# A constant starting address for the second block's activations, with 260 columns in its mixing and gate/value products

## What is computed

```
# block one, 256 positions
h    = rms_norm(x, norm1_w)
proj = h @ w_in                        # "in1": q, k, v, z, xbc, dt
x   += concat(attention, ssm) @ w_out  # "out1"
x   += conv_ffn(rms_norm(x, norm2_w))  # "ffn1": w_up 2048 x 11264, w_down 5632 x 2048
# block two, 16 meta positions ahead of the 256: 272 positions
z    = rmsnorm(h, g_pre_mix) @ w_in_2  # "in2"
mix  = concat(short_conv(z), rwkv7_scan(z)) @ w_out_2     # "out2"
h    = h + rmsnorm(mix, g_post_mix)
gate, up = split(rmsnorm(h, g_pre_ffn) @ w_gate_up)       # "ffn2"
f    = (silu(conv3(gate)) * up) @ w_down
out  = (h + rmsnorm(f, g_post_ffn))[:, 16:]
```

## Time and profile before

| | |
|---|---|
| runs | 2490.72, 2490.09, 2489.69 us; median 2490.09 |
| profiled execution | 2490.57 us, of which the instructions span 2488.8 us |
| TensorE matmul / weight load busy | 2470.6 us (99%) / 2379.1 us (96%) |
| VectorE / ScalarE / GpSimd busy | 1662.9 us (67%) / 1205.5 us (48%) / 59.5 us (2%) |
| granted TensorE clock | 0.999 of full speed |

### The profile page before, as it was taken

The page is one execution under the profiler, slowest core; times in us unless marked ns, Lnnn a source line. Parts: engine busy times, 40 slices in busy tenths (PEclk is TensorE's granted clock), DMA queues, the critical chain, the costliest instruction groups (busy, mean ns, idle before and its releaser), DMA issues.

```text
span 2488.8 us, 61026 instructions
## 1 busy us (share of the span) xinstructions
PE 2470.6 (99%) x25716; PEld 2379.1 (96%) x25716; DVE 1662.9 (67%) x2174; ACT 1205.5 (48%) x1450; POOL 59.5 (2%) x69
## 2 busy tenths in 40 slices
PE   9999999999999999999999999999999999999999
PEld 9989999999999999999999999999999999999997
DVE  7776667677777777788856655667656666556666
ACT  6646545555555555455523333346444444444444
POOL 0000000000000000004100000001000000000000
PEclk9999999999999999999999999999999999999999
DMA  7545556666666665666533333354655555655553
GB/s 229 163 145 156 150 166 191 198 193 193 192 193 191 189 197 187 190 193 176 160 107 103 104 96 105 111 170 153 208 181 185 182 181 176 190 181 185 179 182 129
DMA packets 397851, 420.57 MB, mean 169 GB/s; under 512 B 15422, under 2 KB 372530, under 8 KB 397554
## 3 DMA queue, kind: packets, MB, share of 16 engines
q1 hardware_dynamic: 397170, 416.46, 54.3%
q10 hardware_dynamic: 528, 1.84, 0.2%
HBM read 416.15 MB, written 2.10 MB: 168 GB/s over the span
## 4 chain that ended last, share of the span: by engine, by line
PE 96%; DVE 2%; ACT 1%; issue 1%; POOL 0%; ACTq 0%; POOLq 0%
PE psum L2572 26%; PE psum L2573 26%; PE psum L2574 26%; PE psum L2588 3%; PE psum L2587 3%; PE psum L2586 3%; PE psum L3050 2%; PE psum L3156 1%; PE psum L3146 1%; PE psum L3275 0%; DVE w_lo L1378 0%; PE psum L3197 0%; PE psum L3281 0%; PE psum L2818 0%; PE psum L2997 0%
## 5 line engine op out<-in xcount | busy, mean ns | idle before, releaser
L2572 PE MATMUL psum<-act_hi,w_hi 128*128 128x256 f32 (+3 forms) x4736 | 1350.1, 285 | 3.7 <-DVE act_lo L1416 2.9
L2573 PE MATMUL psum<-act_lo,w_hi 128*128 128x256 f32 (+3 forms) x4736 | 1333.5, 282 | 0.0
L2574 PE MATMUL psum<-act_hi,w_lo 128*128 128x256 f32 (+3 forms) x4736 | 1332.5, 281 | 0.3 <-issue 0.3
L1378 DVE TENSOR_TENSOR w_lo<-raw,w_hi 128x1024 fp32r<-128x1024 f32 x788 | 961.2, 1230 | 475.6 <-ACT w_hi L750 474.5
L750 ACT ACTIVATE w_hi<-raw 128x1024 fp32r<-128x1024 f32 x788 | 829.2, 1057 | 908.5 <-PE psum L2574 764.0
L2572 PEld LDWEIGHTS psum<-act_hi,w_hi 128*128 128x128 f32 x4736 | 894.1, 189 | 12.0 <-issue 3.5
L2573 PEld LDWEIGHTS psum<-act_lo,w_hi 128*128 128x128 f32 x4736 | 895.9, 189 | 3.6 <-issue 2.2
L2574 PEld LDWEIGHTS psum<-act_hi,w_lo 128*128 128x128 f32 x4736 | 894.3, 189 | 0.0
L2573 PE MATMUL psum<-ff_lo_rows,w_hi 128*128 128x256 f32 x640 | 176.8, 276 | 0.0
L2574 PE MATMUL psum<-ff_hi_rows,w_lo 128*128 128x256 f32 x640 | 176.8, 276 | 0.0
L2572 PE MATMUL psum<-ff_hi_rows,w_hi 128*128 128x256 f32 x640 | 176.8, 276 | 0.0
(11 more groups left out here) (431 smaller groups left out, 1926.9 us busy)
## 6 DMA issues: line engine op xcount, KB each, us to landing
raw<-in_w_in SPq DMA_DIRECT2D x188, 512.0 KB, 3.8
raw<-in_w_up SPq DMA_DIRECT2D x176, 512.0 KB, 4.5
raw<-in_w_down SPq DMA_DIRECT2D x176, 512.0 KB, 3.6
raw<-in_w_gate_up SPq DMA_DIRECT2D x176, 512.0 KB, 3.5
raw<-in_w_out SPq DMA_DIRECT2D x64, 512.0 KB, 3.5
x_rows<-in_x SPq DMA_DIRECT2D x8, 256.0 KB, 6.9
out_x<-out_rows SPq DMA_DIRECT2D x8, 256.0 KB, 2.6
raw<-in_w_in SPq DMA_DIRECT2D x4, 384.0 KB, 3.4
```

The lines of the kernel that those rows point to most:

```text
L1378: dve.tensor_tensor(w_lo[:, slot], raw[:, slot], w_hi[:, slot].bitcast(F32), ALU.subtract).then_inc(S["lo_done"], 1)
L2572: pe.matmul(out_, wh, xh, start=first and r == 0, stop=False)
L2573: pe.matmul(out_, wh, xl, start=False, stop=False)
L2574: mm = pe.matmul(out_, wl, xh, start=False, stop=last and r == RK - 1)
```

## The change

The rows of the activations in block two are put 1280 bytes (320 columns, `ROW2`) apart in buffers of their own, `act2_hi` and `act2_lo`, which start at a multiple of 256. Columns 4 to 275 hold the 272 positions. `LEAD` goes from 2 to 4, so that out2 and ffn2 work on 260 columns, which start at the same byte as in2's 260. The value half of ffn2 reads and computes the same 260 columns; `leave` takes 256 of them out of PSUM at an offset of 4. in1 and ffn1 share buffers `act1_hi` and `act1_lo` with rows 1024 bytes apart, begun at 64. The activations of the feed-forward parts all start at the head of their buffers. To find the room, `p1` to `p4` become one tile that is updated in place, and eight small tiles of the scan (`l2`, `l2t`, `l4`, `l4t`, `l8`, `lp`, `pn`, `tt`) lie in the 48 unused columns behind each activation row, so that their four pieces of 32 columns are 1280 bytes apart and no longer joined. No wait is added or taken away, and no instruction either.

```diff
-    LEAD = 2
+    LEAD = 4
...
+    ROW2 = 320
...
-    act_hi = sb("act_hi", [P, KD * T2 + 64], F32R)
-    act_lo = sb("act_lo", [P, KD * T2 + 64], F32R)
...
-    IN1_HI, IN1_LO = act_rows(44, T1)
-    FFN1_HI, FFN1_LO = act_rows(48, T1)
-    IN2_HI, IN2_LO = act_rows(4, T2)
-    MIX_HI, MIX_LO = [t[:, :, 0:T3] for t in act_rows(0, T2)]
...
+    sb("act_pad", [P, 56])
+    block1 = ExitStack()
+    M.update(shared([("act1_hi", [KD * T1 + 64], F32R), ("act1_lo", [KD * T1 + 64], F32R)], block1))
...
-         ("ssm_pad", [40], F32), ("ssm_hi", [8, T1], F32R), ("ssm_lo", [8, T1], F32R)],
+         ("ssm_pad", [48], F32), ("ssm_hi", [8, T1], F32R), ("ssm_lo", [8, T1], F32R)],
...
+    block2 = ExitStack()
+    M.update(shared([("act2_hi", [KD, ROW2], F32R), ("act2_lo", [KD, ROW2], F32R)]))
+    M.update(shared([("gap_hi", [KD, ROW2], F32), ("gap_lo", [KD, ROW2], F32)], block2))
...
-    FF_AT = dict(ffn1=0, ffn2=32)
...
-    LAST_HI, LAST_LO = [M[t][:, 2:2 + 4 * T1].rearrange("p (k t) -> p k t", t=T1)
-                        for t in ("last_hi_rows", "last_lo_rows")]
+    def act_rows(name):
+
+        return M[name][:, 16:16 + KD * T1].rearrange("p (k t) -> p k t", t=T1)
+
+    IN1_HI, IN1_LO = act_rows("act1_hi"), act_rows("act1_lo")
+    FFN1_HI, FFN1_LO = IN1_HI, IN1_LO
+    IN2_HI, IN2_LO = M["act2_hi"][:, :, 4:4 + T2], M["act2_lo"][:, :, 4:4 + T2]
+    MIX_HI, MIX_LO = IN2_HI[:, :, TC3], IN2_LO[:, :, TC3]
...
+    for at, names in enumerate((("l2", "l2t", "l4", "l4t"), ("l8", "lp", "pn", "tt"))):
+        for g, n in enumerate(names):
+            M[n] = M[("gap_hi", "gap_lo")[at]][:, 4 * g:4 * g + 4, 4 + T2:4 + T2 + RC]
...
-            def bank_pair(pair, T, rows_=P):
-                return psum[0:rows_, 2 * pair:2 * pair + 2, 0:T]
+            def bank_pair(pair, T, rows_=P, at=0):
+                return psum[0:rows_, 2 * pair:2 * pair + 2, at:at + T]
...
-                vals = [t[:, :, T - T1:T] for t in xs]
...
-                        if by_rows and j >= 2:
-                            group(v + 4 * j, g + j, (pair0 + j) % 2, vals, T1)
-                        else:
-                            group(v + 4 * j, g + j, (pair0 + j) % 2, xs, T)
+                        group(v + 4 * j, g + j, (pair0 + j) % 2, xs, T)
...
-                        unit(u + 12 + k, k, 3, *vals, 4 * k, T1, k == 0, k == 3)
+                        unit(u + 12 + k, k, 3, *xs, 4 * k, T, k == 0, k == 3)
...
-                    dve.tensor_tensor(M["p2"][0:RB], four(4, 2 * P), M["p1"][0:RB], ALU.add) \
+                    dve.tensor_tensor(M["p"][0:RB], four(4, 2 * P), M["p"][0:RB], ALU.add) \
```

More of the change, by code:

```diff
@@ L275, in two_blocks @@
     first.close()
+    block1.close()
+    block2 = ExitStack()
+    M.update(shared([("act2_hi", [KD, ROW2], F32R), ("act2_lo", [KD, ROW2], F32R)]))
+    M.update(shared([("gap_hi", [KD, ROW2], F32), ("gap_lo", [KD, ROW2], F32)], block2))
+    for names in (
+        [("packs", [NPACK, P], F32), ("x_rows", [2, D], F32), ("meta_rows", [D], F32)],
+        [
+            ("up", [8, T3], F32), ("conv", [8, T1], F32), ("ff", [4, T1], F32),
+            ("squares2", [8, T2], F32), ("row_pad", [48], F32),
+            ("ff_hi_rows", [4 * T1 + 64], F32R), ("ff_lo_rows", [4 * T1 + 64], F32R),
+            ("last_hi_rows", [4 * T1 + 64], F32R), ("last_lo_rows", [4 * T1 + 64], F32R),
+            ("out_rows", [2, D], F32),
+            ("row_ss", [2, 8], F32),
+        ],
+    ):
+        M.update(shared(names))
     both = ExitStack()
@@ L284, in two_blocks @@
     M.update(shared([
-        *[(n, [4, RC], F32) for n in ("ldt", "lo", "rbt0", "rbt1", "akt", "rkt0", "rkt1", "ld", "l2", "l2t", "l4",
-                                      "l4t", "l8", "p1", "p2", "p3", "p4", "lp", "pn", "tt")],
+        *[(n, [4, RC], F32) for n in ("ldt", "lo", "rbt0", "rbt1", "akt", "rkt0", "rkt1", "ld", "p")],
         ("rhs", [4, P], F32), ("trb", [12 * RC], F32),
@@ L297, in two_blocks, with rows_of_four @@
     both.close()
-    FF_AT = dict(ffn1=0, ffn2=32)
[L301 to L305, removed]
-    LAST_HI, LAST_LO = [M[t][:, 2:2 + 4 * T1].rearrange("p (k t) -> p k t", t=T1)
-                        for t in ("last_hi_rows", "last_lo_rows")]
+    block2.close()
+    def act_rows(name):
[4 more added lines that the diff above has]
+    MIX_HI, MIX_LO = IN2_HI[:, :, TC3], IN2_LO[:, :, TC3]
+    NORM_HI = dict(n0=IN1_HI, n1=FFN1_HI, n2=IN2_HI, n4=MIX_HI)
+    NORM_LO = dict(n0=IN1_LO, n1=FFN1_LO, n2=IN2_LO, n4=MIX_LO)
+    for at, names in enumerate((("l2", "l2t", "l4", "l4t"), ("l8", "lp", "pn", "tt"))):
+        for g, n in enumerate(names):
+            M[n] = M[("gap_hi", "gap_lo")[at]][:, 4 * g:4 * g + 4, 4 + T2:4 + T2 + RC]
+    def rows_of_four(name):
+        return M[name][:, 0:4 * T1].rearrange("p (k t) -> p k t", t=T1)
+    FF_HI, FF_LO = rows_of_four("ff_hi_rows"), rows_of_four("ff_lo_rows")
+    LAST_HI, LAST_LO = rows_of_four("last_hi_rows"), rows_of_four("last_lo_rows")
     proj = M["proj"]
@@ L1020, in while_up @@
                     hi_group(v + 8)
-                    product_hi(i - 1, v, ff_rows(name)[0])
+                    product_hi(i - 1, v, FF_HI)
                     hi(v + 12, 0)
@@ L1383, in lo_group, with leave @@
                     lo(u + j, j)
-            def bank_pair(pair, T, rows_=P):
-                return psum[0:rows_, 2 * pair:2 * pair + 2, 0:T]
-            def leave(u_end, pair, dst, T, rows_=P, how="scaled", single=False, t0=0):
+            def bank_pair(pair, T, rows_=P, at=0):
+                return psum[0:rows_, 2 * pair:2 * pair + 2, at:at + T]
+            def leave(u_end, pair, dst, T, rows_=P, how="scaled", single=False, t0=0, at=0):
                 dve.wait_ge(S["unit_used"], u_end)
-                src = bank_pair(pair, T, rows_)
+                src = bank_pair(pair, T, rows_, at)
                 if single:
@@ L1884, in while_up @@
                             taps(i, 2 * j - 2, 2)
-                    product_lo(i - 1, *ff_rows(name))
+                    product_lo(i - 1, FF_HI, FF_LO)
                     leave_up(v, 2)
@@ L2373, in stage @@
                     dve.wait_ge(*own_at("p2", i))
-                    dve.tensor_tensor(M["p3"][0:RB], four(4, P), M["p2"][0:RB], ALU.add) \
+                    dve.tensor_tensor(M["p"][0:RB], four(4, P), M["p"][0:RB], ALU.add) \
                         .then_inc(done_at, 1)
@@ L2378, in stage @@
                     dve.wait_ge(*own_at("p3", i))
-                    dve.tensor_tensor(M["p4"][0:RB], four(4, 0), M["p3"][0:RB], ALU.add) \
+                    dve.tensor_tensor(M["p"][0:RB], four(4, 0), M["p"][0:RB], ALU.add) \
                         .then_inc(done_at, 1)
@@ L2953, in ffn @@
                     ups(u + 24 * i - 8, gp * i - (gp - 4) + g0)
-                    downs(u + 24 * i + 8, gp * i - (gp - 8) + g0, i - 1, *ff_rows(name))
+                    downs(u + 24 * i + 8, gp * i - (gp - 8) + g0, i - 1, FF_HI, FF_LO)
                 if by_rows:
@@ L3234, in early @@
                         pe.wait_ge(S["v_made"], 2 * q + 2)
-                    each_tile(done, M["lo"], tile_of("p4"), 4, 0)
-                    each_tile(done, M["p4"], lambda s, h: M["ident32"][s], 4, P)
+                    each_tile(done, M["lo"], tile_of("p"), 4, 0)
+                    each_tile(done, M["p"], lambda s, h: M["ident32"][s], 4, P)
                     turned(done, q, tt, Z_V, 4, 256)
```

29 lines of the change are left out of this document (6 added, 23 removed).

## The result

The kernel after runs in 2475.51 us (median of 5, 2475.33 to 2478.08), the kernel before in 2490.72 us (5 runs, 2489.69 to 2492.34). The ratio is 0.9941, with a 95% interval from 0.9926 to 0.9955: 15 us faster, 0.6%. The forecast was 44.4 us of gain. The sign and the range held; the size was three times too large, and rival A's 2474 us came closest.

The account below looks back on a forecast made before the run. TensorE, busy 99% of the span, was taken as the bound, so only matmul spacing counts. Terms 16.7 + 14.2 + 8.1 + 4.1 + 1.3 = 44.4 us took 2490.57 us, less 0.48, to 2446 us; range 2434 to 2480.

Parts of the forecast that it names:

- rival A: Anything wider than 256 columns keeps its price, 12 to 13 ns above its columns; 15.3 us gain, 2474 us; chance 0.34.
- What bounds the kernel: Whole kernel: TensorE busy 99% of the span, so time is the number of matmuls by the spacing of their starts.
- I take the lower one: Out2 and ffn2's gate half: 260 columns at constant 64 take 115.0 ns, gaining 16.7 us; value half likewise, 14.2 us.
- The second products: ffn2's turned 512-column downs, 960 matmuls, activations moved from 192 to 64: taken as 0, up to 2.4 us either way.
- in1: Block one, start 48 becomes 64: 2124 matmuls at 115.5 ns, 8.1 us gain, between 3.4 and 12.7.
- Rival C: ffn1 loses its 113.3 ns level as buffers move, 117.8 side at 117.7: 27 us dearer, 2501 or 2473 us; chance 0.08.
- The last chunk of ffn1: Start 72 becomes 64 in ffn1's last chunk: 192 matmuls gain 6.7 ns each, 1.3 us.
- the 260s: in2's 260-column groups, 1632 matmuls at some 120.0 ns: half of a possible 8.2 us taken, 4.1 us gain.
- The 272s: in2's 272-column groups, 864 matmuls, start stays 16 past a multiple of 64: taken as 0, +4.4 to -0.8 us.
- Rival B: Width alone decides spacing and the start does nothing: wider products make it 5.9 us slower, 2496 us; chance 0.04.
- The weight load: Matmul streams: loading weights isn't what holds spacing at 113.3 ns, since identity products with 128-column loads follow every 109 ns.

Follow-up runs that it names:

- a2: Kernel after with 256-column value half at 64, in2's rows at 64, gate and out2 at 48, ffn2's second-product activations at 128: 2460.15 us, ratio to before 0.9878.
- the grid: Two kernels of matmul triplets alone, varying start and width, then also weight place, weight columns and products ahead; 256 columns at 64 took 113.3 or 117.8 ns.
- a1: Kernel after with block two's rows begun at 0 instead of 16 bytes and the value half again 256 columns, begun at 64: 2465.59 us, ratio to before 0.9891.
- a3: Kernel after with one fp32 product, its result unread, ahead of out1's second half: 2477.11 us, ratio 0.9942.
- a4: Kernel after with every buffer from the activations on moved 256 bytes further, weights left in place: 2476.37 us in one run.
- a5: Kernel after with six fp32 products, their results unread, ahead of out1's second half: 2480.17 us against 2492.64 in one run.

## Why the prediction was wrong

**What bounds the kernel, and how to read it: right.** The 15 us are spacings of matmuls, less some longer gaps between stretches (1.5 us in in1). VectorE's and ScalarE's busy times in a chunk of ffn2 (42.0 and 31.5 us) did not move, and at a2's 66.6 us a chunk they still kept up.

**The step that failed: "I take the lower one" for 260 columns at a constant 64.** That put 115.0 ns on 2880 + 2112 matmuls, 30.9 us. Measured: 120.0 ns, so 0.8 x 2880 + 1.7 x 2112 = 5.9 us. I moved a number from 256 columns to 260 because the start was the same. The row that spoke against it was in my hands, 260 columns of which a quarter start at 64 and which average 120.0, and I explained it away by the ssm rows' two levels, as if a stream had to settle. It doesn't: in the kernel before, 48 matmuls in the middle of the ssm stretch that the earlier trace rows shows at 117.7 keep that level,

```profile
342.72:348.38 5.66, 5.66 (x51) 5.66 (x50) 2.49 (x4) 2.88 (x4) 0.00 (x0) 1.00 0.64 197
```

and the next stretch, which begins at 351.05 us behind a break, is at 112 to 114 ns from its fourth matmul on. The grid shows no cheap start for 260 among 15, and in the kernel after all 260-column products, entered in many ways, average 120.0.

**Rival A: the number nearly right, its reason not.** Its 15.3 us of gain come to 2474.8 us, 0.7 us from the measured time, but partly by luck: it had nothing for the second products (4.1 us) and nothing for the losses in out1 and ffn1 (2.4 us). Its price of 12 to 13 ns above the columns for whatever is wider than 256 fails in the grid, where 264 columns at 64 take 120.0 ns, 10 above their 110, and 254 take 118.3, 12.5 above theirs. (The 13.3 ns that the prediction gives the turning 260 are counted from 256 columns; above its own 108.3 ns it has 11.7.)

**The second products: mis-sized.** I put 0, with 2.4 us as the most; it was 4.1 us. The row at 72 (230.8) was taken as the nearest to 64, as if the spacing ran smoothly between starts. It doesn't: 228.9 at 64, 230.7 at 72, 233.3 at 96, 228.3 at 112, 226.7 at 128.

**in1: right, the last digit by luck.** 8.1 us forecast, 8.1 measured, by both levels in one stage as supposed: its long stretch at 113.3, others at 117.8. The mean of 114.7 is below the 115.5 taken and alone would give 9.6 us; 1.5 us went into longer gaps at the breaks.

**What no term held: out1.** Its 384 attention matmuls were entered in the dear level and stayed there, 384 x 4.5 = 1.7 us lost. Rival C had this level, but put it in ffn1 and on the buffers' new places; ffn1's chunks kept 113.3, and whether the places matter in out1 is open. The last chunk of ffn1 fell to 117.4 rather than 113.3, 0.5 us instead of 1.3; in a1, a2 and a3, with the same places there, it ran at 113.5 to 113.9.

**in2: the 4.1 us put down for the 260s never came** (119.9 ns before, 120.0 after), from the same failed step. The 272s gave 0.4 us, put at 0. Rival B is out: wider and faster, 256 to 260 in the value half.

Summed up: 8.1 + 5.9 + 4.1 + 0.5 + 0.4 - 1.7 = 17.3 us by terms. The head of ffn1, entered in out1's dear level, takes 0.7 us of it (4224 matmuls at a mean of 113.5 ns for 113.3). The other 1.5 us down to the span's 15.1 are placed by stage only, not by cause: ffn2 is 0.7 us and in2 with the scan 0.6 us longer than their terms say, and in2's stage varies by more than that by itself.

The weight load isn't as harmless as the prediction read the earlier trace rows: with 32 weight columns the stream at 64 took 120.0 ns and the one at 0 took 115.5.

The Trainium skill (TensorE: Matmul & The Clock Gate, Back-to-back issue gap) gives N / 2.4 + 2.5 ns as the gap of an isolated matmul and says that in a stream of weight loads and matmuls both set the spacing, which the prediction left out. By the formula 256 columns would take 109.2 ns; in the grid they take from 113.3 to 120.0.

## What to carry to other kernels

When a kernel is bound by back-to-back matmuls, measure the time from start to start for each pair of width and starting byte in a kernel of matmuls alone; here such a grid gave the full kernel's numbers back to 0.3 ns, but not which of its two levels a stretch takes, and 50 cases cost one run. Don't carry a good number from one width to another, and don't interpolate between starts: fewer columns at the right byte (256 at 64, 113.3 ns) beat a constant start for wider ones (120.0 ns), and the row that doesn't fit the theory is the one to believe.

## What the runs showed of the hardware that was not expected

- The spacing of fp32r matmuls depends on the distance between the streamed rows' start and the loaded weights' start, modulo 256 bytes in all that was tried. At 256 columns it is 113.3 ns at the distances -64 (117.8 in some entries) and +112, and 116.7 to 120.0 at the others measured, each of these entered in one way. Loading 32 weight columns instead of 128 made the stream at 64 dearer (120.0 ns) and the one at 0 cheaper (118.7 to 115.5).
- 248, 252 and 256 columns at 64 take 113.3 ns, but 250 take 120.0 and 254 take 118.3: of the widths up to 256 tried at this start from 248 on, the two that aren't a multiple of 4 columns are the dear ones.
- The same stream at the same place runs at 113.3 or 117.8 ns from entry on, for hundreds of matmuls. In the grid the number of products ahead changed which, and one stretch of in1 came out at either in two executions.
- The stage with the scan differs from execution to execution, 478.7 to 485.8 us in these profiles, and 479.5 to 485.8 in the four that have the same program and places there (the kernel after, a3, a4 shifted by 256 bytes, a5). The matmuls in it have single gaps of about 1.2 us in varying number (at 1414.56, 1480.40 and 1504.14 us in the kernel before), which the waits file as "issue": time in which TensorE waited for nothing that the profile shows. TensorE's idle time in the stage goes from 5.5 to 8.7 us in these four, about half of the spread; the rest isn't explained. That is why differences of 1 us were read from the other stages here.
